# wo1's half units for both tiles two quarters at a time, and both tiles' sums ahead of the turned copies and the norm

## The chip, the cores and the metric

The kernel runs on one core of a Trainium2 chip. The metric is device time in microseconds, the median of several executions. A core has TensorE (PE, with its weight loads as PEld), VectorE (DVE), ScalarE (ACT), GpSimd (POOL) and SyncE (SP), which here issues nearly all transfers, and 16 DMA engines. Each engine runs its own program in order; they meet at semaphores.

## The reference, cut to what matters

One layer for 256 tokens of width 1024: a norm, one wide projection, three branches (chunked attention, a state-space scan, attention into a memory), their gated sum through `w_out`, and then a mixture of 32 experts, four for each token.

```python
x = x + merged @ w_out[l]
x = x + moe_ffn(rms_norm(x, norm_ffn[l]), w_router[l], b_router[l], w_gate[l], b_gate[l],
                w_up[l], b_up[l], w_down[l], b_down[l])
...
logits = (xt @ w_router + b_router).astype(jnp.float32)
top_val, top_idx = lax.top_k(logits, TOP_K)
wts = jax.nn.softmax(top_val, axis=-1)
...
g = jnp.minimum(xblk @ w_gate[e] + b_gate[e], SWIGLU_LIMIT)
u = jnp.clip(xblk @ w_up[e] + b_up[e], -SWIGLU_LIMIT, SWIGLU_LIMIT)
act = (u + 1.0) * g * jax.nn.sigmoid(SWIGLU_ALPHA * g)
y = act @ w_down[e] + b_down[e]
```

## The kernel before

**Tiles and units.** The 256 tokens are two tiles of 128 rows (`t` = 0, 1). The dense part walks through `BLOCKS`, 512-column blocks of the weights, each cut into four quarters of 256 input rows. A quarter is a unit `w`. For each unit ScalarE rounds the weights to a high part (L713), VectorE takes the rest (L1026), and TensorE multiplies in three passes, high by high, low by high, high by low (`three_passes`, L1597 to L1599), two input chunks for each tile. So a quarter is 6 matmuls of 128x512 per tile. `splits` holds four units in turn. The last two blocks, `("wo", 0)` and `("wo", 1)`, are the halves of `merged @ w_out`.

**The order.** `schedule()` writes one list of steps, `SCHED`; every engine walks through it and does the steps it knows. `at(w, ...)` puts a step behind unit `w`'s matmuls and the split of unit `w` + 3. What comes behind the list is written out by hand for each engine ("the tail").

**The seam.** Of the block wo1, TensorE does only tile 0 inside the list (`last_block`). Behind the third quarter the step `outT` turns the first half of `x_sb` (8 transposes of 128x128, L1584), behind the fourth `logits` does the first half of the router's product for both tiles (L1604), with the router matrix scaled on VectorE (L1370). Then the tail: `second_tile(q)` does tile 1's half units, each counted in `unit_used`; `turn_out(t)` turns the second half of `x_sb` for tile t; `last_logits(t)` is the second half of the router's product; `open_sum` starts a result bank with `x_sb` (L1871); `gather(t0, t1)` collects the rows of the next expert (L1864), and the counting matmuls (L1886, L1891, L1899, L1903) give each token its place.

**VectorE's tail.** `add_out(t)` adds wo1's product to `x_sb` (L1412), `take_xT(t)` copies the turned half (L1418), `norm_begin(t)` sums two partial squares and forms the variance (L1424, L942), ScalarE takes the root (`root`, L681), `choose(t)` finishes the inverse root in five small operations (L950 to L954), takes the logits (L1432) and the four largest, and `find_first(t)` marks the rows of expert 0 (L1449, L1451). Tile 0 goes through most of this before tile 1's sum is added. ScalarE forms the partial squares (L884) and the normed rows `h2` (L890, two halves for each tile), in the order tile 0, tile 1.

**The banks.** `group()` hands out three banks in turn for transposes and small products; TensorE may fill one again when VectorE has taken what was in it three groups ago.

**The experts.** 32 experts, each with six half-loads of 2 MB: gate 0 and 1, up 2 and 3, down 4 and 5. Ten slots hold them in turn; most slots lie over memory of the dense part. SyncE issues in order: expert 0's six during the dense part, then these:

```python
sp.wait_ge(unit_used, UNITS - 2)
expert_load(1, 0)
sp.wait_ge(unit_used, UNITS)
expert_load(1, 1)
expert_load(1, 2)
sp.wait_ge(sem("logits_ready"), TT)
sp.wait_ge(sem("h2_ready"), 2 * TT)
sp.wait_ge(sem("x_opened"), 2 * TT)
expert_load(1, 3)
```

Every later load (L515 on the queue) waits until TensorE has used what the slot held; the down half 4 of expert 0 frees the slot for the third load of expert 2. `expert()` on TensorE runs gate, scatter of the expert before, up (L1936 for both), gather for the next one, then down (L1974).

Of the kernel before, what the change touches and what calls it, by code (L numbers as in the profile page):

```python
# [92 lines left out]
def schedule():  # L93
# [110 lines left out]
    at(first("wo", 1) + 2, "outT")  # L204
    at(first("wo", 1) + 3, "logits")
# [45 lines left out]
def hybrid_block_kernel(nc, x, mem, g_mix, w_in, w_dt, a_gains, rel_rev, conv_w, conv_b, dt_bias, a_log, d_skip,  # L251
                        g_ssm, g_mem, w_mem_kv, x_gains, w_br_a, w_br_b, w_br_c, w_out, norm_ffn, w_router,
                        b_router, w_gate, b_gate, w_up, b_up, w_down, b_down, bias_dram, out):
    with ExitStack() as ctx:
# [420 lines left out]
        def _(act):  # L675
# [28 lines left out]
            for step in SCHED:  # L704
# [28 lines left out]
                elif kind == "take" and step[1] == "wo":  # L733
                    i = step[2]
                    cols = slice(i * NB, (i + 1) * NB)
                    for h in range(2):
# [3 lines left out]
                            .then_inc(sem("out_squares"), 1)  # L740
                elif kind == "take" and step[1:] != ("bc", 1):
# [139 lines left out]
            for t in range(TT):  # L881
# [4 lines left out]
                root(1)  # L886
                act.wait_ge(sem("second_norm"), t + 1)
# [33 lines left out]
        def _(dve):  # L921
# [39 lines left out]
            def rstd_here(dst, src, width):  # L961
# [12 lines left out]
                return last  # L974

# [17 lines left out]
            for step in SCHED:  # L993
# [366 lines left out]
                elif kind == "take" and step[1] == "wo":  # L1360
# [4 lines left out]
                    for h in range(2):  # L1365
                        n = GEMM_AT[("wo", i, h)]
                        dve.tensor_tensor(x_sb[:, h, cols], x_sb[:, h, cols], ps[:, GEMM_BANKS[n % 4], :], ALU.add)\
                            .then_inc(gemm_taken, 1)
                    dve.wait_ge(gain2_landed, 32)
                    dve.tensor_tensor(wr_sb[:], wr_sb[:], gain2_sb[:].unsqueeze(2).to_broadcast([P, KC, EXPERTS]),  # L1370
                                      ALU.mult).then_inc(sem("router_scaled"), 1)
                elif kind == "outT":
                    for c2 in range(2):
# [29 lines left out]
            across = [P, TOP_K, EXPERTS]  # L1403

            def add_out(t):

                n = GEMM_AT[("wo", 1, t)]
                if t == 0:
                    dve.wait_ge(sem("wo_first_tile"), 1)
                else:  # L1410
                    dve.wait_ge(unit_used, UNITS)
                dve.tensor_tensor(x_sb[:, t, NB:2 * NB], x_sb[:, t, NB:2 * NB], ps[:, GEMM_BANKS[n % 4], :], ALU.add)\  # L1412
                    .then_inc(gemm_taken, 1)

            def take_xT(t):

                b = group()
                dve.tensor_copy(xT[:, 4:8, t * P:(t + 1) * P], ps[:, b, :].rearrange("p (c t) -> p c t", c=4))\  # L1418
                    .then_inc(misc_taken, 1)

            def norm_begin(t):

                dve.wait_ge(sem("out_squares"), TT + t + 1)
                link(dve.tensor_tensor(ss_2[:, t:t + 1], ss_part[:, t:t + 1], ss_part[:, TT + t:TT + t + 1], ALU.add))  # L1424
                variance(rs_2[:, t:t + 1], ss_2[:, t:t + 1], D)

            def choose(t):

                inverse_root(rs_2[:, t:t + 1]).then_inc(sem("second_norm"), 1)
                dve.wait_ge(sem("second_norm"), t + 1)  # L1430
# [136 lines left out]
        def _(pe):  # L1567
# [42 lines left out]
            for step in SCHED:  # L1610
# [8 lines left out]
                elif kind == "gemm":  # L1619
# [39 lines left out]
                    if closes:  # L1659
                        n += 2  # L1660
# [405 lines left out]
```

## Time and profile before

| | us |
|---|---|
| median of 3 runs | 1451.22 |
| lowest, highest | 1450.0, 1451.28 |
| profiled execution | 1451.71 |
| its span | 1449.6 |
| TensorE busy in the span | 1425.6 |
| granted TensorE clock, mean | 0.999 |

The span is what the profile's engines cover; 2.1 us of the profiled execution lie around it. Two stages follow each other: the dense part to about 535 us, and the experts, 28.1 us each, to the end. The change lies between them, at 510 to 540 us. A row of the timeline gives the start, the duration, the engine and line, the tiles, how many records are in it, and in brackets the idle time ahead of it with what ended that. A float32 matmul has two records. Ends of matmuls are modelled and overlap, so the pitch, start to start, is what counts.

### The profile page before, as it was taken

The page shows a single profiled execution, that of the slowest core. Times are in us where ns is not written, and L with a number is a line of the kernel's source. Part 1 is how long each engine was busy: PE and PEld are TensorE (multiplying, and loading weights), DVE is VectorE, ACT ScalarE, POOL GpSimd, SP SyncE. Part 2 cuts the span into 40 slices and gives each one's busy share as a digit, 9 for nine tenths or more (in the row PEclk, how much of TensorE's full clock was granted, in tenths as well). Part 3 has the DMA queues.
Part 4 walks back from the last instruction along what each step waited for, and adds up shares of the span by engine and source line. Part 5 has one row for each costly group of instructions (what it writes and reads, how often), then busy time and mean ns, then how long its engine had stood idle before and what let it go on. Part 6 is the DMA issues. An engine that isn't in the chain of part 4 may idle for free.

```text
span 1449.6 us, 18621 instructions
## 1 busy us (share of the span) xinstructions
PE 1425.6 (98%) x7575; PEld 820.6 (57%) x7575; DVE 588.4 (41%) x1149; ACT 405.6 (28%) x601; POOL 63.3 (4%) x50
## 2 busy tenths in 40 slices
PE   6999999999999999999999999999999999999998
PEld 6998888777788864444444444444444444433433
DVE  6779788777788651211112121121212112111211
ACT  5766666556544531101010110110001011001100
POOL 5110000121100000000000000000000000000000
PEclk9999999999999999999999999999999999999999
DMA  8455544555474979999999999999999999999996
GB/s 251 156 189 174 162 136 162 194 161 169 166 272 144 365 300 417 428 428 428 427 429 429 430 427 429 428 430 428 430 427 430 428 428 429 429 429 428 429 428 287
DMA packets 74000, 491.27 MB, mean 339 GB/s; under 512 B 5264, under 2 KB 8976, under 8 KB 49376
## 3 DMA queue, kind: packets, MB, share of 16 engines
q1 hardware_dynamic: 71280, 487.57, 83.3%
q10 hardware_dynamic: 2160, 2.62, 0.6%
q8 instruction: 32, 0.52, 0.2%
q0 software_dynamic: 512, 0.43, 0.1%
q14 instruction: 16, 0.13, 0.0%
HBM read 488.93 MB, written 1.07 MB: 338 GB/s over the span
## 4 chain that ended last, share of the span: by engine, by line
PE 84%; DMA 10%; DVE 4%; ACT 1%; issue 1%; DVEq 0%; SPq 0%; ACTq 0%
PE ps L1936 26%; PE ps L1974 13%; PE ps L1597 8%; PE ps L1599 8%; PE ps L1598 8%; PE ps L1864 7%; DMA regions<-in_w_up 6%; PE ps L1584 4%; PE ps L1916 4%; DMA regions<-in_w_gate 3%; DVE regions L1172 1%; DVE splits L1026 1%; PE ps L1811 1%; PE ps L1944 1%; DMA halves<-in_w_in 1%
## 5 line engine op out<-in xcount | busy, mean ns | idle before, releaser
L1936 PE MATMUL ps<-regions,sig 128*64 128x512 f32 x2048 | 463.3, 594 | 4.8 <-DMA regions<-in_w_gate 4.6
L1936 PEld LDWEIGHTS ps<-regions,sig 128*64 128x64 f32 x2048 | 141.8, 137 | 277.6 <-issue 259.2
L1974 PE MATMUL ps<-regions,tmp 128*64 128x512 f32 x1024 | 225.1, 592 | 0.0
L1597 PE MATMUL ps<-splits,regions_r 128*128 128x512 f32 x512 | 205.8, 402 | 0.1
L1599 PE MATMUL ps<-splits,regions_r 128*128 128x512 f32 x512 | 200.1, 391 | 0.0
L1598 PE MATMUL ps<-splits,regions_r 128*128 128x512 f32 x512 | 199.8, 390 | 0.0
L713 ACT ACTIVATE splits<-halves 128x1024 fp32r<-128x1024 f32 x152 | 159.1, 1056 | 96.4 <-PE ps L1599 81.6
L1026 DVE TENSOR_TENSOR splits<-halves,splits 128x1024 fp32r<-128x1024 f32 x132 | 162.0, 1232 | 44.1 <-ACT splits L713 42.7
L899 ACT ACTIVATE work<-work 128x512 f32<-128x512 f32 x32 | 20.1, 629 | 475.8 <-DVE work L1524 475.8
L1974 PEld LDWEIGHTS ps<-regions,tmp 128*64 128x64 f32 x1024 | 71.7, 137 | 132.0 <-issue 129.6
L1864 PEld LDWEIGHTS ps<-craw,regions 128*128 128x128 f32 x1024 | 119.2, 192 | 25.6 <-issue 25.2
L1864 PE MATMUL ps<-craw,regions 128*128 128x64 f32 x1024 | 124.7, 275 | 0.4 <-DVE craw L1451 0.4
L1529 DVE TENSOR_SCALAR work<-ps 128x512 f32<-128x512 f32 x32 | 22.1, 691 | 239.8 <-PE ps L1936 239.8
L1597 PEld LDWEIGHTS ps<-splits,regions_r 128*128 128x128 f32 x512 | 96.2, 188 | 22.4 <-issue 3.9
L1599 PEld LDWEIGHTS ps<-splits,regions_r 128*128 128x128 f32 x512 | 96.1, 188 | 20.9
L1538 DVE COPY sig<-ps 128x512 f32<-128x512 f32 x32 | 22.1, 692 | 211.1 <-PE ps L1974 211.1
L1598 PEld LDWEIGHTS ps<-splits,regions_r 128*128 128x128 f32 x512 | 96.3, 188 | 18.4
L904 ACT ACTIVATE tmp<-ps 128x512 f32<-128x512 f32 x32 | 19.1, 597 | 303.1 <-PE ps L1584 303.1
L1524 DVE TENSOR_SCALAR work<-ps 128x512 f32<-128x512 f32 x32 | 22.1, 691 | 177.7 <-PE ps L1936 177.7
L1916 PE MATMUL ps<-sig,craw 64*128 64x512 f32 x264 | 65.6, 615 | 0.8 <-DVE sig L1538 0.8
L668 POOL TENSOR_TENSOR splits<-halves,splits 128x1024 fp32r<-128x1024 f32 x20 | 48.7, 2433 | 328.7 <-ACT splits L713 328.7
L1597 PE MATMUL ps<-regions_r,splits 128*128 128x256 f32 x192 | 55.3, 288 | 0.0
(299 smaller groups left out, 1188.1 us busy)
## 6 DMA issues: line engine op xcount, KB each, us to landing
regions<-in_w_gate SPq DMA_DIRECT2D x64, 2048.0 KB, 30.1
regions<-in_w_up SPq DMA_DIRECT2D x64, 2048.0 KB, 28.4
regions<-in_w_down SPq DMA_DIRECT2D x64, 2048.0 KB, 31.2
halves<-in_w_in SPq DMA_DIRECT2D x48, 1024.0 KB, 5.2
halves<-in_w_br_b SPq DMA_DIRECT2D x8, 1024.0 KB, 5.1
halves<-in_w_mem_kv SPq DMA_DIRECT2D x8, 1024.0 KB, 5.1
halves<-in_w_br_a SPq DMA_DIRECT2D x4, 1024.0 KB, 5.1
halves<-in_w_br_c SPq DMA_DIRECT2D x4, 1024.0 KB, 7.5
```

The source lines that it names most:

```text
L668: pool.tensor_tensor(lo, raw, hi.bitcast(F32), ALU.subtract).then_inc(lo_ready_pool, 1)
L713: act.activation(hi, raw, ACT.Copy).then_inc(hi_ready, 1)
L1026: dve.tensor_tensor(lo, raw, hi.bitcast(F32), ALU.subtract).then_inc(lo_ready, 1)
L1524: dve.tensor_scalar(g_sb, ps[:, G_BANK, :], LIMIT, None, ALU.min).then_inc(sem("g_ready"), 1)
L1584: return pe.transpose(dst, src, ident[:])
L1597: pe.matmul(out, lhs[0], rhs[0], start=start, stop=False, skip_group_check=True)
L1598: pe.matmul(out, lhs[1], rhs[0], start=False, stop=False, skip_group_check=True)
L1599: return pe.matmul(out, lhs[0], rhs[1], start=False, stop=stop, skip_group_check=True)
L1864: last = pe.matmul(ps[:, X_BANK, c * BLK:(c + 1) * BLK], h2[:, t, c * P:(c + 1) * P], hot[:, t], start=(t == 0 and c == 0), stop=(t == TT ...
L1916: last = pe.matmul(ps[:, ACC[2 * t + h], :], hot_wT[rows, t], yb[rows], start=False, stop=False, skip_group_check=True)
L1936: last = pe.matmul(ps[64 * h:64 * h + 64, bank, :], xgT[:, 4 * k + c], eslots[slot][:, c, h * NB:(h + 1) * NB], start=(k == 0 and c == 0), ...
L1974: last = pe.matmul(ps[64 * h:64 * h + 64, D_BANK, :], actT[:, c, 64 * k:64 * k + 64], eslots[slot][:, c, h * NB:(h + 1) * NB], start=False ...
```

## The change

In `schedule()` the half units of wo1's tile 1 enter the list, two behind the second quarter and two behind the fourth. `outT` and `logits` move behind all of wo1, and `outT` now also turns the second half for both tiles. The router scaling becomes a step of its own, earlier. `picks` on ScalarE gets a root of one column, whose result is not used. VectorE adds both tiles' sums first, then takes four copies, then finishes both norms, then chooses. ScalarE writes the normed rows behind both roots. On TensorE the second half of tile 1's logits waits until tile 0's are taken. SyncE's code is the same.

```diff
-    at(first("wo", 1) + 2, "outT")
-    at(first("wo", 1) + 3, "logits")
+    for q in range(2):
+        at(first("wo", 1) + 1, "second", q)
+        at(first("wo", 1) + 3, "second", q + 2)
+    at(UNITS, "outT")
+    at(UNITS, "logits")
+    at(first("bc", 0) + 1, "router_scale")
...
+                elif kind == "picks":
+
+                    act.activation(root_out[:, 31:32], ident[:, 0:1], ACT.Sqrt).then_inc(sem("root_warm"), 1)
...
                 root(1)
+            for t in range(TT):
                 act.wait_ge(sem("second_norm"), t + 1)
...
                 elif kind == "outT":
+                    add_out(0)
+                    norm_begin(0)
+                    add_out(1)
...
-            add_out(0)
             take_xT(0)
-            norm_begin(0)
+            take_xT(1)
+            norm_end(0)
+            norm_begin(1)
+            norm_end(1)
             choose(0)
-            add_out(1)
-            take_xT(1)
-            norm_begin(1)
             find_first(0)
             choose(1)
...
+                    turn_out(0)
+                    turn_out(1)
...
-            second_tile(0)
-            turn_out(0)
-            second_tile(1)
             last_logits(0)
-            second_tile(2)
-            second_tile(3)
-            pe.wait_ge(gemm_taken, GEMM_AT[("wo", 1, 0)] + 1)
+            pe.wait_ge(gemm_taken, GEMM_END)
             open_sum(0, 0)
-            turn_out(1)
+            pe.wait_ge(sem("logits_taken"), 1)
+            last_logits(1)
...
-            pe.wait_ge(gemm_taken, GEMM_END)
             open_sum(1, 0)
-            last_logits(1)
```

`norm_end(t)` is the inverse root that stood at the head of `choose(t)`.

On TensorE, from the last matmul of wo1 to the first gather and a little past it. `splits` are the weights, `ident` marks transposes and opened sums, `wr_sb` the router, `chosen_r` the counting, `craw` the gathers. Before:

```order
L1599 MATMUL ps<-splits,regions_r 128x512
L1871 MATMUL ps<-regions,ident 128x512
L1584 MATMUL ps<-ident,regions 128x128 x4
L1886 MATMUL ps<-chosen_r,upto_r 128x32
L1871 MATMUL ps<-regions,ident 128x512
L1604 MATMUL ps<-wr_sb,regions 128x32 x4
L1891 MATMUL ps<-chosen_r,ones_r 128x32
L1864 MATMUL ps<-craw,regions 128x64 x8
L1871 MATMUL ps<-regions,ident 128x512
L1899 MATMUL ps<-chosen_r,upto_r 128x32
```

and now:

```order
L1614 MATMUL ps<-splits,regions_r 128x512
L1599 MATMUL ps<-ident,regions 128x128 x16
L1619 MATMUL ps<-wr_sb,regions 128x32 x12
L1890 MATMUL ps<-regions,ident 128x512
L1619 MATMUL ps<-wr_sb,regions 128x32 x4
L1901 MATMUL ps<-chosen_r,upto_r 128x32
L1890 MATMUL ps<-regions,ident 128x512
L1904 MATMUL ps<-chosen_r,ones_r 128x32
L1883 MATMUL ps<-craw,regions 128x64 x8
L1890 MATMUL ps<-regions,ident 128x512
L1912 MATMUL ps<-chosen_r,upto_r 128x32
```

All transposes and router matmuls but the last group now stand behind the last wo1 matmul, where before a part of them stood between the quarters; tile 1's last router group has moved ahead of the first count.

On VectorE, from the copies of the picks on, behind the last split. `regions<-regions,ps` are the sums, `regions<-ps` the turned copies, `stat` the norm, `rt` the logits. Before:

```order
L1348 COPY cbm<-ident 32x128 x3
L1375 COPY regions<-ps 128x512 x2
L1412 TENSOR_TENSOR regions<-regions,ps 128x512
L1418 COPY regions<-ps 128x4x128
L1424 TENSOR_TENSOR stat<-stat 128x1
L942 TENSOR_SCALAR stat<-stat 128x1
L950 RECIPROCAL stat<-stat 128x1
L951 TENSOR_TENSOR stat<-stat 128x1
L952 TENSOR_TENSOR stat<-stat 128x1
L953 TENSOR_SCALAR stat<-stat 128x1
L954 TENSOR_TENSOR stat<-stat 128x1
L1432 SCALAR_TENSOR_TENSOR rt<-ps,stat,head_rows 128x32
```

and now:

```order
L1385 COPY cbm<-ident 32x128 x3
L993 TENSOR_TENSOR regions<-regions,ps 128x512
L1005 TENSOR_TENSOR stat<-stat 128x1
L950 TENSOR_SCALAR stat<-stat 128x1
L993 TENSOR_TENSOR regions<-regions,ps 128x512
L1417 COPY regions<-ps 128x512 x2
L999 COPY regions<-ps 128x4x128 x2
L958 RECIPROCAL stat<-stat 128x1
L959 TENSOR_TENSOR stat<-stat 128x1
L960 TENSOR_TENSOR stat<-stat 128x1
L961 TENSOR_SCALAR stat<-stat 128x1
L962 TENSOR_TENSOR stat<-stat 128x1
```

Both sums are ahead of all four copies, tile 0's inverse root is behind them, and tile 1's norm (another seven rows like these) comes before the first logits are taken.

On ScalarE, from the squares of wo0 on. Before:

```order
L739 ACTIVATE tmp,stat<-regions 128x512 x2
L884 ACTIVATE tmp,stat<-regions 128x512
L681 ACT_TABLE_LOAD
L681 ACTIVATE stat<-stat 128x1
L890 ACTIVATE regions<-regions,stat 128x512 x2
L884 ACTIVATE tmp,stat<-regions 128x512
L681 ACTIVATE stat<-stat 128x1
L890 ACTIVATE regions<-regions,stat 128x512 x2
```

and now:

```order
L743 ACTIVATE tmp,stat<-regions 128x512 x2
L747 ACT_TABLE_LOAD
L747 ACTIVATE stat<-ident 128x1
L891 ACTIVATE tmp,stat<-regions 128x512
L685 ACTIVATE stat<-stat 128x1
L891 ACTIVATE tmp,stat<-regions 128x512
L685 ACTIVATE stat<-stat 128x1
L898 ACTIVATE regions<-regions,stat 128x512 x4
```

The table load stands ahead of wo1's squares instead of behind them, and both roots are ahead of all four writes of normed rows.

## Rows read from the trace of the kernel before

**Rows 1.** Page, parts 1 and 2: busy us and count; GB/s moved, in 40 slices

```profile
PE 1425.6 (98%) x7575; PEld 820.6 (57%) x7575; DVE 588.4 (41%) x1149; ACT 405.6 (28%) x601; POOL 63.3 (4%) x50
...
GB/s 251 156 189 174 162 136 162 194 161 169 166 272 144 365 300 417 428 428 428 427 429 429 430 427 429 428 430 428 430 427 430 428 428 429 429 429 428 429 428 287
```

**Rows 2.** Page, part 5: busy us, mean ns, idle before and its releaser

```profile
L1936 PE MATMUL ps<-regions,sig 128*64 128x512 f32 x2048 | 463.3, 594 | 4.8 <-DMA regions<-in_w_gate 4.6
```

**Rows 3.** Chain that ended last: start us, us, what

```profile
1384.67 43.48 DMA regions<-in_w_up
```

**Rows 4.** Windows: us, PE, PEld, DVE, ACT, POOL busy, PEclk, DMA share, GB/s

```profile
520.00:522.00 2.00, 2.00 (x15) 1.73 (x13) 1.32 (x6) 0.20 (x1) 0.00 (x0) 1.00 0.00 0
562.00:563.00 1.00, 1.00 (x8) 0.39 (x6) 0.00 (x0) 0.00 (x0) 0.00 (x0) 1.00 0.80 295
```

**Rows 5.** Timeline of SyncE's DMA queue: start us, us, engine, line, transfer

```profile
521.70 3.96 SPq L515 DMA_DIRECT2D regions<-in_w_gate  x2
...
535.11 0.33 SPq L515 DMA_DIRECT2D regions<-in_w_up  x1
...
560.89 0.33 SPq L515 DMA_DIRECT2D regions<-in_w_up  x1
...
589.02 0.33 SPq L515 DMA_DIRECT2D regions<-in_w_up  x1
```

**Rows 6.** DMA view, 521 to 523, 535 to 536, 560 to 561: us to landing

```profile
regions<-in_w_gate SPq DMA_DIRECT2D x1, 2048.0 KB, 7.6
...
regions<-in_w_up SPq DMA_DIRECT2D x1, 2048.0 KB, 9.7
...
regions<-in_w_up SPq DMA_DIRECT2D x1, 2048.0 KB, 9.3
```

**Rows 7.** Timeline of PE, 510 to 535: start us, us, line, idle before

```profile
510.17 0.39 PE L1597 MATMUL ps<-splits,regions_r 128*128 128x512 f32 x1
...
514.02 0.39 PE L1599 MATMUL ps<-splits,regions_r 128*128 128x512 f32 x1
...
514.25 1.03 PE L1584 MATMUL ps<-ident,regions 128*128 128x128 f32 x8
...
524.91 0.40 PE L1599 MATMUL ps<-splits,regions_r 128*128 128x512 f32 x1
...
525.14 1.02 PE L1871 MATMUL ps<-regions,ident 128*128 128x512 f32 x2
...
527.61 1.05 PE L1604 MATMUL ps<-wr_sb,regions 128*128 128x32 f32 x8
...
528.61 1.98 PE L1864 MATMUL ps<-craw,regions 128*128 128x64 f32 x16
...
532.11 2.00 PE L1864 MATMUL ps<-craw,regions 128*128 128x64 f32 x16 [0.37 <-DVE craw L1451]
```

**Rows 8.** Timeline of DVE, 514 to 532, same columns

```profile
514.89 1.29 DVE L1375 COPY regions<-ps 128x512 f32<-128x512 f32 x2
...
525.34 0.69 DVE L1412 TENSOR_TENSOR regions<-regions,ps 128x512 f32<-128x512 f32 x1 [0.99 <-PE ps L1599]
...
527.45 0.15 DVE L1424 TENSOR_TENSOR stat<-stat 128x1 f32<-128x1 f32 x1
...
528.11 0.15 DVE L950 RECIPROCAL stat<-stat 128x1 f32<-128x1 f32 x1
...
529.07 0.25 DVE L1432 SCALAR_TENSOR_TENSOR rt<-ps,stat,head_rows 128x32 f32<-128x32 f32 x1
...
530.42 0.39 DVE L1442 TENSOR_REDUCE chosen_r<-work 128x32 fp32r<-128x128 f32 x1
...
531.58 0.19 DVE L1449 TENSOR_TENSOR rt<-ps,chosen_r 128x32 f32<-128x32 f32 x1 [0.70 <-PE ps L1899]
```

**Rows 9.** Timeline of ACT, 521 to 525, same columns

```profile
521.29 0.20 ACT L681 ACTIVATE stat<-stat 128x1 f32<-128x1 f32 x1 [1.85 <-DVE stat L942]
...
522.49 2.31 ACT L890 ACTIVATE regions<-regions,stat 128x512 f32<-128x512 f32 x2 [1.00 <-DVE stat L954]
```

More of the change, by code:

```diff
@@ L974, in rstd_here, with add_out, take_xT, norm_begin @@
                 return last
+            across = [P, TOP_K, EXPERTS]
+            def add_out(t):
+                n = GEMM_AT[("wo", 1, t)]
+                if t == 0:
+                    dve.wait_ge(sem("wo_first_tile"), 1)
+                else:
+                    dve.wait_ge(unit_used, UNITS)
+                dve.tensor_tensor(x_sb[:, t, NB:2 * NB], x_sb[:, t, NB:2 * NB], ps[:, GEMM_BANKS[n % 4], :], ALU.add)\
+                    .then_inc(gemm_taken, 1)
+            def take_xT(t):
+                b = group()
+                dve.tensor_copy(xT[:, 4:8, t * P:(t + 1) * P], ps[:, b, :].rearrange("p (c t) -> p c t", c=4))\
+                    .then_inc(misc_taken, 1)
+            def norm_begin(t):
+                dve.wait_ge(sem("out_squares"), TT + t + 1)
+                link(dve.tensor_tensor(ss_2[:, t:t + 1], ss_part[:, t:t + 1], ss_part[:, TT + t:TT + t + 1], ALU.add))
+                variance(rs_2[:, t:t + 1], ss_2[:, t:t + 1], D)
+            def norm_end(t):
+                inverse_root(rs_2[:, t:t + 1]).then_inc(sem("second_norm"), 1)
+                dve.wait_ge(sem("second_norm"), t + 1)
             dve.wait_ge(sem("masks"), 3)
@@ L1368, in _ @@
                             .then_inc(gemm_taken, 1)
+                elif kind == "router_scale":
                     dve.wait_ge(gain2_landed, 32)
@@ L1400, in _ @@
                             .then_inc(sem("br_merged"), 1)
[L1403 to L1425, printed above, removed]
             def choose(t):
-                inverse_root(rs_2[:, t:t + 1]).then_inc(sem("second_norm"), 1)
-                dve.wait_ge(sem("second_norm"), t + 1)
                 dve.wait_ge(sem("logits_ready"), t + 1)
@@ L1606, in router, with second_tile, turn_out @@
                 return last
+            def second_tile(q):
+                w = first("wo", 1) + q
+                hi, lo = quarter(w)[1:]
+                b = GEMM_BANKS[GEMM_AT[("wo", 1, 1)] % 4]
+                for c in range(2):
+                    k = 2 * q + c
+                    last = three_passes(ps[:, b, :], (mergedT[0][:, k, P:T], mergedT[1][:, k, P:T]),
+                                        (hi[:, c], lo[:, c]), k == 0, k == KC - 1)
+                last.then_inc(unit_used, 1)
+            def turn_out(t):
+                b = group()
+                pe.wait_ge(gemm_taken, GEMM_AT[("wo", 1, t)] + 1)
+                for c in range(4):
+                    last = turn(ps[:, b, c * P:(c + 1) * P], x_sb[:, t, (4 + c) * P:(5 + c) * P])
+                last.then_inc(misc_ready, 1)
             pe.wait_ge(sem("masks"), 3)
@@ L1660, in _ @@
                         n += 2
+                elif kind == "second":
+                    second_tile(step[1])
                 elif kind == "headT":
```

15 lines of the change are left out of this document (removed).

## The prediction

> **What bounds the kernel now.** I read the page first: TensorE is busy nearly all the time, and in the second half the 16 DMA engines carry 425 to 430 GB/s without a break [rows 1]. Both look full, so the share of busy time decides nothing, and the waits have to. The group of first-layer expert matmuls (L1936) sat idle for 4.6 us on transfers of w_gate [rows 2], and the chain that ended last passes through a transfer of w_up that takes 43.48 us from issue to landing [rows 3]. So the last experts wait for weights.
>
> Pace explains it. The third half-transfer of w_up's expert 2 lands at 560.89 + 9.3 = 570.2, and 175 transfers later expert 31's lands at 1384.67 + 43.48 = 1428.15 [rows 3, 5, 6]: 857.95 / 175 = 4.90 us each, 29.4 us for an expert's six. TensorE takes 589.02 - 560.89 = 28.13 us an expert [rows 5]. It starts with weights in store, gains 1.3 us per expert on the transfers, and runs out near the end. From there the end is the end of the transfer stream, and TensorE has about 4.6 us in hand. The question for any edit ahead of the experts is therefore when the stream last had nothing to do.
>
> The windows give two such places [rows 4]: nothing moves at 520 to 522, because the first load of expert 1 waits for the last quarters of wo1 and is issued at 521.70, its follower 3.6 us later [rows 5]; and a dip to 295 GB/s at 562 to 563. The dip belongs to the load issued at 560.89, when expert 0's down half frees its slot; it lands 9.3 us later, where a load that meets idle engines lands in 7.6 [rows 5, 6]. So before, the stream is all but caught up with TensorE at that point.
>
> **Part 1: the wo1 quarters.** The same 48 matmuls run. Their pitch is (514.02 - 510.17) / 17 = 0.2265 us [rows 7]. Before, 18 of them, then transposes and router matmuls stand between the rest, and the last starts at 524.91 [rows 7]. Now nothing stands between: the 24th ends at 510.17 + 23 x 0.2265 + 0.39 = 515.8, the 48th at 510.17 + 47 x 0.2265 + 0.39 = 521.2. The input is there: VectorE split the last quarter before it added wo0's sums, ahead of its copies at 514.89 [rows 8]. So the first load of expert 1 goes out at 515.8 instead of 521.70, 5.9 us earlier, and the next two at about 521.3 instead of 525.4. The fourth (k = 3) still waits for both tiles' logits, the normed rows and the opened sums, as at 535.11 before [rows 5].
>
> **Part 2: the chain from the sums to the first gather.** VectorE adds tile 1 at 521.25 (0.03 us after the last matmul, as at 525.34 before [rows 7, 8]). Then come four copies at the pitch of the pair at 514.89, 0.60 us, so the reciprocal of tile 0 starts at 521.25 + 5 x 0.60 = 524.3. It does not wait for its root. Before, ScalarE had idled for 1.85 us ahead of the root at 521.29, waiting for the variance [rows 9], so the table load ahead of that was hidden; now the load stands behind the squares of wo0, and the root is done near 520.6. Removing that load is thus worth nothing on the path. The norm of tile 0 takes 529.07 - 528.11 = 0.96 us to its end [rows 8], so tile 1's begins at 525.3; its sum-to-next step takes 529.07 - 527.45 = 1.62, so the first logits are taken at 526.9 (TensorE's first logits are ready at about 525.9: eight transposes 0.9, eight more 0.9 with a wait of 0.2 for the first copy, then router matmuls in three groups like the one of eight records, 0.9 each [rows 7]). From there the choice takes 530.42 + 0.39 - 529.07 = 1.74, to 528.6. TensorE has meanwhile waited for the taken logits (527.15) and done the second half of tile 1's (0.85, to 528.0), and now waits for the choice. Its counting matmul (0.25), then find-first, 532.11 - 531.58 = 0.53 [rows 7, 8], would give 529.45; the opened sum behind the counting matmul (0.9 [rows 7]) holds the queue to 529.7. So the first gather starts at 529.7 against 528.61 on its row, or 528.76 by the chain of waits: **1.0 us later**.
>
> Queued behind it on TensorE are an opened sum, the second count and the second gather. Tile 1's choice ends at 531.1, so it hides under the first gather and the sum behind it; the second gather comes 0.95 us later than its 532.11 [rows 7]. ScalarE's normed rows, 2.31 us for one tile [rows 9], now run as four in a row from 525.9 to 530.5, ahead of both gathers. All that follows (the gathered rows, weights, number of passes) hangs on the second gather, as before. Expert 0 and its freed slots shift by +1.0. The router scale, 0.4 us of VectorE, moves to a stretch where it waits for its next split; it had no one waiting before and has none now: 0.
>
> The bounds of this term: TensorE's own work from 521.1 to the gather adds to 7.2 us, which would end at 528.3, so the chain can cost -0.4 at the least. At the most, some eight hand-overs between engines that I priced at 0.03 to 0.1 us each cost 0.2 more each, which makes +2.6. I take +1.0, the sum.
>
> **Part 3: the transfers.** After the change, with issue times as above: expert 1's loads land at 515.8 + 7.6 = 523.4, then 521.3 + 7.6 = 528.9, then about 534. The fourth is issued at 536.1 and meets idle engines: 543.7, where it landed at 535.11 + 9.7 = 544.8 before [rows 5, 6]. So 5.9 us of an earlier start shrink to 1.1 here. The next ones follow at 4.90: 548.6, 553.5, 558.4, 563.3. The load of 560.89 is now issued at 561.9; the engines are free for it at 563.3 and it lands no sooner than 561.9 + 7.6 = 569.5 (back to back it would be 568.2). Before: 570.2. **Gain 0.7 us.** Later loads have margin: the next of this kind is issued 28.1 us later and comes to a stream that has gained backlog 1.3 us per expert. The end follows the stream: -0.7. In general it is the shift of TensorE less 1.7.
>
> The fixed part of a lone load is 7.6 - 4.90 = 2.7 us here. The Trainium skill, "DMA: Bandwidth & Descriptors", section "Anatomy of one DMA", puts it at some 2.0 us, measured on the path issued by GpSimd; by that the stream would gain 1.4 us instead of 0.7. The row decides, and these loads are issued by SyncE.
>
> **Sum.** Profiled execution 1451.71 us, span 1449.6, so 2.1 lies around it; the profiled execution stands 0.5 above the median 1451.22. Span 1449.6 - 0.7 = 1448.9; on the median, 1451.2 - 0.7 = **1450.5 us**. About 0.2% (2.9 us) is what a measurement of this kernel can tell from no change.
>
> **Rivals.**
> 1. TensorE's lateness counts in full: the earlier loads bring nothing, because the stream at the dip is paced by slots alone and the 1.7 us between 9.3 and 7.6 is how the engines drain, not a queue. The end is then +1.0: 1452.2. For it: the dip is soft, 295 GB/s and not zero. Chance 0.10, still within 0.2%.
> 2. The stream keeps the whole 5.9 us: 1445.3. That wants no new gap ahead of the fourth load and none at the slots of expert 0. Against it: both those issues hang on TensorE, which is no earlier. Partial forms of it need a seam 2 us or more shorter than my sum. Chance 0.08.
> 3. Slower: TensorE's clock falls in the seam. The change adds waits of about 0.9 and 0.6 us, in 8 us, to an engine that had none there before the 0.37 at 532.11 [rows 7]. If it fell from 2.4 to 1.2 GHz ahead of the gathers, two gathers and the sum between them, 1.85 + 0.9 + 2.0 = 4.7 us, would take twice that, TensorE would be 5.7 late, and the end 5.7 - 1.7 = +4.0: 1455.2. It decides from a lateness of 1.7 us for the sign and 4.6 for a measurable loss. Against it: the granted clock is 1.00 in the windows on both sides of the present waits [rows 4]. Chance 0.06, with the rest of what can hold the chain up by that much. The Trainium skill, "TensorE: Matmul & The Clock Gate", section "What's actually happening", says that the clock is throttled unless activity releases it; by that rule this is the case to look for.
>
> **How the numbers follow.** The forecast has 0.76, rival 1 has 0.10, rival 2 0.08, rival 3 0.06. Faster by over 0.2% is rival 2: 0.08. Slower is rival 3: 0.06. Within 0.2% is the rest: 0.86. The bounds -0.4 and +2.6 of the chain give -2.1 and +0.9 at the end, 1449.1 to 1452.1; the spread of the runs before, 1450.0 to 1451.28, and rival 1 widen this to 1448.6 to 1452.8, which leaves out rivals 2 and 3, less than 2 in 10.
>
> **What would show it.** The first load of expert 1 goes out near 515.8 and its two followers near 521.3; the DMA windows then show a new hole around 534 to 537 and a deeper one at 563; the first gather starts near 529.7 with two waits of TensorE ahead of it, for taken logits and for the choice; the pick wait of expert 0 shifts by 1.0; idle time of L1936 on w_gate shrinks from 4.6 to about 3. I am wrong if the first gather is earlier than 528 or later than 532, if the stream has no hole ahead of the fourth load, or if the clock leaves 1.00.

## The result: no gain, and two kinds of execution

| | before | after |
|---|---|---|
| median of 20 runs, us | 1450.93 | 1457.93 |
| lowest, highest | 1449.48, 1452.83 | 1450.35, 1461.44 |
| profiled execution, its span | 1451.71, 1449.6 | 1457.58, 1455.5 |
| granted TensorE clock of the profiled execution | 0.999 | 0.994 |

The ratio is 1.0036, with a 95% interval from 1.0025 to 1.0047: slower by 0.36%, clear of the noise. The ratio does not follow the medians, because the 20 runs of after are of two kinds. Seven lie between 1450.35 and 1451.44, all with a granted clock of 1.000. Thirteen lie between 1456.76 and 1461.44, all at 0.993 to 0.995. Nothing lies between. The 20 runs of before have no second kind. Three executions of the sets behind the experiments (5166.63 us in experiment 5, and 6081.64 and 8331.11 of the kernel before) took several times as long, with a granted clock of 1.0, and are left out below.

The page of after, parts 1, 2 and 5, beside [rows 1, 2]: busy time; granted clock in tenths and GB/s in 40 slices; the first expert matmuls (L1949 now) with their idle time.

```profile
PE 1432.9 (98%) x7575; PEld 826.7 (57%) x7575; DVE 588.2 (40%) x1149; ACT 405.8 (28%) x602; POOL 63.9 (4%) x50
...
PEclk9999999999999979999999999999999999999999
...
GB/s 246 158 189 173 164 136 163 189 165 174 154 271 159 356 235 422 426 430 426 431 426 430 426 430 427 430 427 429 428 428 429 428 429 427 430 427 430 427 429 297
...
L1949 PE MATMUL ps<-regions,sig 128*64 128x512 f32 x2048 | 463.5, 594 | 3.7 <-DMA regions<-in_w_gate 3.4
```

Busy time of TensorE is up by 7.3 us for the same 7575 matmuls. They did not become more, they became slower: the clock's row has a 7 in one slice, and the 15th of the GB/s row is 235 where [rows 1] have 300. The wait for w_gate, 4.6 us in [rows 2], is 3.4.

Windows of after around that slice: stretch, its length, busy time and count of PE, PEld, DVE, ACT, POOL, granted clock, DMA share, GB/s.

```profile
521.50:526.50 5.00, 4.93 (x42) 4.47 (x41) 4.26 (x13) 1.15 (x4) 0.00 (x0) 1.00 1.01 390
526.50:543.50 17.00, 16.84 (x56) 12.10 (x57) 7.12 (x34) 6.94 (x7) 0.00 (x0) 0.50 0.39 166
543.50:548.50 5.00, 5.00 (x26) 1.59 (x24) 2.84 (x16) 0.00 (x0) 0.00 (x0) 0.98 0.86 301
```

Full clock to about 526.6, half clock (1.2 instead of 2.4 GHz) for 17 us, full clock again near 543.7, once the wide expert matmuls had begun at 543.17. In the first window TensorE was busy for 4.93 of 5.00 us. What it did then is in the timeline of PE: start, duration, line, tiles, records.

```profile
521.54 2.20 PE L1599 MATMUL ps<-ident,regions 128*128 128x128 f32 x16
...
523.68 2.87 PE L1619 MATMUL ps<-wr_sb,regions 128*128 128x32 f32 x24
...
526.38 1.81 PE L1890 MATMUL ps<-regions,ident 128*128 128x512 f32 x2
...
527.98 1.76 PE L1619 MATMUL ps<-wr_sb,regions 128*128 128x32 f32 x8
...
531.68 3.65 PE L1883 MATMUL ps<-craw,regions 128*128 128x64 f32 x16
...
537.75 3.68 PE L1883 MATMUL ps<-craw,regions 128*128 128x64 f32 x16 [0.16 <-DVE craw L1467]
...
543.17 3.90 PE L1949 MATMUL ps<-regions,sig 128*64 128x512 f32 x16
```

Transposes and router matmuls of 32 columns from 521.54 to the opened sum at 526.38, then the fall, ahead of both places where the change makes TensorE wait. In this trace neither wait leaves it idle: the slowed opened sum lasts to about 527.98, past the taking of the logits (527.28 + 0.25), and the choice, done at 528.99, is there before the count at 529.54. So here the fall can't come from the two added waits. The first gather takes 3.65 where [rows 7] have 1.98, the second 3.68 instead of 2.00.

VectorE (DVE) in the same stretch: second sum, first reciprocal, first logits taken, end of the first choice.

```profile
521.74 0.69 DVE L993 TENSOR_TENSOR regions<-regions,ps 128x512 f32<-128x512 f32 x1 [0.90 <-PE ps L1614]
...
524.74 0.15 DVE L958 RECIPROCAL stat<-stat 128x1 f32<-128x1 f32 x1
...
527.28 0.25 DVE L1448 SCALAR_TENSOR_TENSOR rt<-ps,stat,head_rows 128x32 f32<-128x32 f32 x1
...
528.62 0.37 DVE L1458 TENSOR_REDUCE chosen_r<-work 128x32 fp32r<-128x128 f32 x1
```

The transfers: SyncE's queue, the landing of the load at 568.37, and the last w_up transfer of the chain.

```profile
516.28 5.77 SPq L519 DMA_DIRECT2D regions<-in_w_gate  x2
...
522.10 21.56 SPq L519 DMA_DIRECT2D regions<-in_w_up  x2
...
568.37 0.33 SPq L519 DMA_DIRECT2D regions<-in_w_up  x1
...
regions<-in_w_up SPq DMA_DIRECT2D x1, 2048.0 KB, 8.1
...
1390.53 43.48 DMA regions<-in_w_up
```

The first load goes out at 516.28, against 521.70 in [rows 5]; the fourth (the second of the pair that begins at 522.10 and lasts 21.56) near 543.3, against 535.11. Expert 0's freed slot comes at 568.37 instead of 560.89, 7.5 us late, and the last w_up lands at 1434.01 instead of 1428.15, 5.9 us late. The span grew by 5.9.

### The profile page after: what moved, and what is told of

Read it like the earlier page. It is cut to its first block, busy times and chain, and to the rows that moved or that the text cites. A ratio compares the mean times of both kernels' runs of the same rounds, so it can differ in the third digit from the quotient of the medians.

```text
span 1455.5 us, 18623 instructions
## 1 busy us (share of the span) xinstructions
PE 1432.9 (98%) x7575; PEld 826.7 (57%) x7575; DVE 588.2 (40%) x1149; ACT 405.8 (28%) x602; POOL 63.9 (4%) x50
## 4 chain that ended last, share of the span: by engine, by line
PE 85%; DMA 9%; DVE 4%; ACT 1%; issue 1%; ACTq 0%
PE ps L1949 26%; PE ps L1987 14%; DMA regions<-in_w_up 9%; PE ps L1612 8%; PE ps L1614 8%; PE ps L1613 8%; PE ps L1883 8%; PE ps L1599 4%; PE ps L1929 4%; DVE regions L1209 1%; DVE splits L1063 1%; PE ps L1847 1%; PE ps L1957 1%; PE ps L1980 1%; PE ps L1890 0%
## 5 line engine op out<-in xcount | busy, mean ns | idle before, releaser
L1949 PE MATMUL ps<-regions,sig 128*64 128x512 f32 x2048 | 463.5, 594 | 3.7 <-DMA regions<-in_w_gate 3.4
L1949 PEld LDWEIGHTS ps<-regions,sig 128*64 128x64 f32 x2048 | 142.1, 137 | 276.8 <-issue 261.3
L1883 PEld LDWEIGHTS ps<-craw,regions 128*128 128x128 f32 x1024 | 122.5, 196 | 25.9 <-issue 25.7
L1883 PE MATMUL ps<-craw,regions 128*128 128x64 f32 x1024 | 128.1, 279 | 0.2 <-DVE craw L1467 0.2
```

What stands on the lines that cost most here:

```text
L1883: last = pe.matmul(ps[:, X_BANK, c * BLK:(c + 1) * BLK], h2[:, t, c * P:(c + 1) * P], hot[:, t], start=(t == 0 and c == 0), stop=(t == TT ...
L1949: last = pe.matmul(ps[64 * h:64 * h + 64, bank, :], xgT[:, 4 * k + c], eslots[slot][:, c, h * NB:(h + 1) * NB], start=(k == 0 and c == 0), ...
```

## Experiments

The causes tested are called N, W and D in the expectations, and a fourth, L, comes in behind experiment 4. A filler is a matmul that nobody needs, put in only to give TensorE work. N: transposes and narrow matmuls for 4.9 us without wide ones take the clock down. W: the added waits of TensorE do. D: the earlier transfers do. Every median below stands beside runs of the kernel before on the same chip (1451.29 for experiments 1 to 4, 1451.38 for 5 to 8, 1451.30 for 9 to 12).

**1. Waits filled with wide matmuls**

```diff
             open_sum(0, 0)
+            filler()
             pe.wait_ge(sem("logits_taken"), 1)
             last_logits(1)
+            filler()
```

> The changed kernel with one more 512-column float32 matmul (a product nobody reads, into the bank of the last opened sum) in each of TensorE's two new waits, ahead of the one for tile 0's taken logits and ahead of the one for the choice. Theory N: TensorE's clock falls because transposes and 32-column router matmuls run for 4.9 us (521.5 to 526.4) with nothing wide between; both fillers stand behind that, so most executions still fall, median 1457 to 1461. Rival W: the waits make it fall; then the clock stays at 1.00 in all, median 1450.5 to 1452.

Measured: 1452.41 (11 runs, 1451.5 to 1454.44). Six at 1.000, 1451.5 to 1452.41, and five at 0.999, 1453.83 to 1454.44; none like the thirteen of after. The profiled one is of the six. Timeline of PE, then a window:

```profile
523.15 2.87 PE L1619 MATMUL ps<-wr_sb,regions 128*128 128x32 f32 x24
...
526.80 1.02 PE L1895 MATMUL ps<-regions,ident 128*128 128x512 f32 x2
...
528.47 1.10 PE L1895 MATMUL ps<-regions,ident 128*128 128x512 f32 x2
...
530.40 1.98 PE L1883 MATMUL ps<-craw,regions 128*128 128x64 f32 x16
...
524.00:534.00 10.00, 9.63 (x59) 7.14 (x58) 6.19 (x34) 6.12 (x7) 0.00 (x0) 1.00 0.86 369
```

The narrow stretch is that of after. As written, N has failed and W has not, but the five that take 2 us more are foreseen by neither; experiment 6 offers an explanation.

**2. The narrow stretch broken up by wide matmuls**

```diff
+                    filler()
                     turn_out(0)
                     turn_out(1)
...
-                    for t in range(TT):
-                        router(t, 0)
+                    filler()
+                    router(0, 0)
+                    filler()
+                    router(1, 0)
```

> The changed kernel with three such wide matmuls (two records of 0.45 us each) inside the narrow stretch: behind the eight transposes of outT, ahead of tile 0's and ahead of tile 1's first router group. Nothing is taken out, 2.7 us of work are added. Theory N: clock 1.00 in all executions; the seam is 1.5 to 2 us later than that of a changed kernel at full clock, so 1452 to 1454, yet some 5 us below the changed kernel's median 1457.9. Rival W: the wait for the choice is still there, so the clock falls as often and the median is 1459 or more.

Measured: 1453.2 (11 runs, 1451.93 to 1453.79), all at 1.000. One window over the seam:

```profile
521.00:531.00 10.00, 9.77 (x61) 7.27 (x59) 7.16 (x31) 6.43 (x8) 0.00 (x0) 1.00 0.99 406
```

2.7 us of needless work, and the median is 4.7 us below after's. N foresaw this, W did not, though the fillers also shorten the waits behind them, so that this run alone does not exclude W.

**3. TensorE's part of the change alone**

```diff
-    at(first("wo", 1) + 2, "outT")
-    at(first("wo", 1) + 3, "logits")
+    for q in range(2):
+        at(first("wo", 1) + 1, "second", q)
+        at(first("wo", 1) + 3, "second", q + 2)
+    at(UNITS, "outT")
+    at(UNITS, "logits")
...
                         by_columns(lambda t: x_sb[:, t], c2)
+                    turn_out(0)
...
-            second_tile(0)
-            turn_out(0)
-            second_tile(1)
             last_logits(0)
-            second_tile(2)
-            second_tile(3)
```

> The kernel before with TensorE's part of the change alone: tile 1's half units two by two behind the second and fourth quarter, then the transposes and router matmuls of the first half, tile 0's second half and its last router group, and only then an opened sum and tile 1's second half. VectorE and ScalarE keep their order. The narrow stretch is 3.9 us instead of 4.9. Theory N: the clock falls in some or most executions, those at 1456 or more, the others near 1451. Rival W: no wait for the taken logits is added, so the clock stays at 1.00. Rival D: it is the earlier start of the transfers (518 instead of 522) that takes the clock down; then it falls here too, as often as in the changed kernel.

Measured: 1459.06 (6 runs, 1455.59 to 1463.03); all six fell, three at 0.997 and three at 0.992. Timeline of PE with the idle time in brackets, then a window of the fall:

```profile
524.58 0.63 PE L1587 MATMUL ps<-ident,regions 128*128 128x128 f32 x4 [1.75 <-DVE regions L1415]
...
525.04 3.19 PE L1607 MATMUL ps<-wr_sb,regions 128*128 128x32 f32 x24
...
530.80 1.09 PE L1587 MATMUL ps<-ident,regions 128*128 128x128 f32 x4 [0.70 <-DVE regions L1415]
...
528.00:534.00 6.00, 5.29 (x14) 2.72 (x13) 4.00 (x18) 2.94 (x5) 0.00 (x0) 0.50 0.90 385
```

This order has waits of its own, 1.75 and 0.70 us for sums, which my expectation for W had overlooked. It tells that the change's order on TensorE, without VectorE's, is enough for a fall, not by which of the two ways.

**4. VectorE's and ScalarE's part, quarters interleaved as before**

```diff
-    for q in range(2):
-        at(first("wo", 1) + 1, "second", q)
-        at(first("wo", 1) + 3, "second", q + 2)
-    at(UNITS, "outT")
-    at(UNITS, "logits")
+    at(first("wo", 1) + 2, "outT")
+    at(first("wo", 1) + 3, "logits")
...
-                    add_out(0)
-                    norm_begin(0)
-                    add_out(1)
...
+            add_out(0)
+            norm_begin(0)
             take_xT(0)
+            add_out(1)
             take_xT(1)
...
-                    turn_out(0)
-                    turn_out(1)
...
+            second_tile(0)
+            turn_out(0)
+            second_tile(1)
+            second_tile(2)
             last_logits(0)
+            second_tile(3)
+            turn_out(1)
```

> The changed kernel's order on VectorE and ScalarE (both sums early, all turned copies, both roots, then both choices), with tile 1's half units put back between the transposes and router matmuls as before the change. Theory N: clock 1.00 in all, median 1450 to 1452. Rival W: TensorE still waits for tile 0's taken logits and for the choice, so the clock falls in most and the median is 1457 or more. Rival D: the transfers start as late as before the change, so no fall.

Both sums stand in the tail again, and tile 0's turned half is copied between them, so VectorE's order is the changed one only from the second sum on. Measured: 1460.54 (5 runs, 1459.27 to 1463.15), all at 0.994 or 0.995. The same views:

```profile
526.83 0.63 PE L1596 MATMUL ps<-ident,regions 128*128 128x128 f32 x4 [0.87 <-DVE regions L990]
...
530.95 1.08 PE L1616 MATMUL ps<-wr_sb,regions 128*128 128x32 f32 x8 [2.63 <-DVE rt L1442]
...
532.51 0.25 PE L1902 MATMUL ps<-chosen_r,upto_r 128*128 128x32 f32 x1 [0.48 <-DVE chosen_r L1452]
...
534.00:547.00 13.00, 12.85 (x44) 8.96 (x45) 5.48 (x27) 2.83 (x4) 0.00 (x0) 0.50 0.44 168
```

Here the wide matmuls stand between the narrow ones to 525.9, and the clock falls near 533.7, behind waits of 0.87, 2.63 and 0.48 us. So the clock also falls without the narrow stretch, in a seam with long waits, which N does not say. D is out: the first load of expert 1 goes out at 522.34, no earlier than before.

A fourth theory was made to allow for all this, and is called L: in narrow matmuls and in waits alike TensorE does little wide work, and the clock follows the two together.

**5. The waits filled with narrow matmuls**

Here `filler()` is four matmuls of 32 columns.

```diff
             open_sum(0, 0)
+            filler()
             pe.wait_ge(sem("logits_taken"), 1)
             last_logits(1)
+            filler()
```

> The changed kernel with its two new waits filled again, this time with four 32-column matmuls each (eight records, about 0.85 us, the length of the wide filler used before; their product is read by nobody). Neither wait is idle, but nothing wide is added. Theory L (the fall follows how much wide matmul work TensorE does in the seam, and waits and narrow matmuls count alike against it): the clock falls as without fillers, median 1457 to 1461. Rival W (idle time alone takes it down): the clock stays at 1.00 as with the wide fillers, median 1451 to 1453.

Measured: 1461.23 (11 runs, 1451.96 to 1464.68). Four at 1.000, 1451.96 to 1452.48, and seven at 0.991 to 0.993, 1461.22 to 1464.68. Windows, then the two fillers:

```profile
521.50:526.50 5.00, 4.93 (x42) 4.38 (x40) 4.09 (x12) 0.88 (x4) 0.00 (x0) 1.00 1.00 374
...
527.50:547.50 20.00, 19.84 (x72) 15.25 (x72) 7.24 (x32) 6.22 (x7) 0.00 (x0) 0.50 0.30 129
...
527.80 1.76 PE L1896 MATMUL ps<-wr_sb,regions 128*128 128x32 f32 x8
...
531.08 1.89 PE L1896 MATMUL ps<-wr_sb,regions 128*128 128x32 f32 x8
```

Same places as the fillers of experiment 1, no idle time left there, and seven of eleven executions are like the thirteen of after, where experiment 1 had none. In the profiled one the clock falls near 527.4, ahead of the first filler. So W is out for the order of the change: neither here nor in after does an added wait stand ahead of the fall. The Trainium skill, "TensorE: Matmul & The Clock Gate", section "What's actually happening", says that activity releases the throttle. The trace agrees only if activity is something else than the busy time of the profile, which is 4.93 of 5.00 us ahead of this fall too.

**6. One wide filler, in the first wait**

```diff
             open_sum(0, 0)
+            filler()
             pe.wait_ge(sem("logits_taken"), 1)
```

> The changed kernel with one wide 512-column float32 filler, ahead of the wait for tile 0's taken logits; the wait for the choice stays. Theory L: half the cure; executions are mixed, some fallen (1456 or more) and some not (1451 to 1452). If the first wait alone is the cause, none falls; if the second is, as many fall as in the changed kernel, 13 in 20.

Measured: 1453.3 (11 runs, 1450.95 to 1454.04): four at 1.000, 1450.95 to 1452.27, seven at 0.999, 1452.99 to 1454.04. The profiled one, of the seven, inside its fall:

```profile
527.00:530.00 3.00, 3.00 (x7) 1.33 (x5) 1.79 (x9) 3.00 (x4) 0.00 (x0) 0.50 1.02 437
```

The clock fell as in after, near 526.7 and ahead of the filler, and came back near 530 instead of at the experts. I had expected executions at 1456 or more; none came. This tells two things apart. **How often** the clock falls does not visibly change with fillers behind the narrow stretch: 13 of 20 in after, 5 of 11, 7 of 11 and 7 of 11 in experiments 1, 5 and 6, if the five of experiment 1 are read as short falls. None of those five was profiled, and their 0.999 is no sign of it: the profiled execution of before has 0.999 too, from its last stretch, 1440 to 1450 us, where the clock's mean is 0.89. What marks the five is their time. Only the fillers inside the stretch, experiment 2, brought it to 0 of 11. That fits N for the beginning of the fall in this order. **How long** it lasts goes with what comes next: with a second wide matmul beside the opened sum, 1 and 6, it costs 2 us; with a narrow one, 5, or none, after, 6 to 13.

**7. The opened sums moved into the seam**

```diff
+                    open_sum(0, 0)
                     turn_out(0)
                     turn_out(1)
...
-                    for t in range(TT):
-                        router(t, 0)
+                    router(0, 0)
+                    open_sum(1, 0)
+                    router(1, 0)
...
             last_logits(0)
-            pe.wait_ge(gemm_taken, GEMM_END)
-            open_sum(0, 0)
+            open_sum(0, 1)
...
-            open_sum(1, 0)
...
             gather(0, 1)
-            open_sum(0, 1)
+            open_sum(1, 1)
...
             gather(1, 2)
-            open_sum(1, 1)
```

> The changed kernel with its own four opened sums (wide matmuls that it has to do in any case) moved into the seam: one behind the eight transposes of outT, one between the two first router groups, one ahead of the wait for the taken logits, one behind the first gather. No work is added or taken away. Theory L: clock 1.00 in all, median 1450.3 to 1451.8, and 6 us below the changed kernel. Rival W: the wait for the choice stays, so some executions fall.

Measured: 1455.06 (9 runs, 1452.7 to 1456.7), two at 0.999 and seven at 0.995 to 0.997. Missed: I had looked at the first light stretch only. Timeline of PE and a window:

```profile
526.47 1.10 PE L1644 MATMUL ps<-regions,ident 128*128 128x512 f32 x2
...
529.45 2.00 PE L1890 MATMUL ps<-craw,regions 128*128 128x64 f32 x16 [0.46 <-DVE craw L1467]
...
531.29 1.88 PE L1644 MATMUL ps<-regions,ident 128*128 128x512 f32 x2
...
532.00:541.00 9.00, 7.98 (x29) 5.23 (x29) 4.38 (x22) 1.28 (x1) 0.00 (x0) 0.50 0.63 237
```

The sums taken forward are missing behind the first choice. Between the sum at 526.47 and the next one at 531.29 there are only narrow matmuls and waits of 0.24 and 0.46, and the clock falls at 531.4 instead of 526.6. The light stretch had been moved, not removed. The nine at 0.995 to 0.999 end 1.3 to 5.3 us above the kernel before; only this one of them was profiled.

**8. The kernel before, with the transfers held back**

```diff
             sp.wait_ge(unit_used, UNITS - 2)
+            sp.wait_ge(sem("logits_ready"), TT)
             expert_load(1, 0)
```

> The kernel before, with SyncE's first load of expert 1 held back until both tiles' logits are there (issued at about 528.7 instead of 521.70). TensorE's order and clock are those of before. Theory S (the stream of transfers, from the last place where it ran dry, sets the end): that load lands at 536.3, the fourth at 551.0 instead of 544.8, and the stream is 6.2 us late from there on: 1457. Rival P (the stream is paced by freed slots alone, and when it starts is of no account): 1451, no change.

Measured: 1457.31 (5 runs, 1456.71 to 1457.89), clock 1.000: +5.9 us, 1457 expected. Issue and landing of the fourth load, and the first expert matmuls:

```profile
535.30 0.33 SPq L515 DMA_DIRECT2D regions<-in_w_up  x1
...
regions<-in_w_up SPq DMA_DIRECT2D x1, 2048.0 KB, 16.8
...
L1937 PE MATMUL ps<-regions,sig 128*64 128x512 f32 x2048 | 463.8, 595 | 8.2 <-DMA regions<-in_w_gate 7.7
```

It lands at 552.1 instead of 544.8, and the experts wait 7.7 us for w_gate instead of 4.6. The stream does set the end, and of the 7.3 us by which that load lands later, 5.9 are paid.

**9. The table load alone, on the kernel before**

```diff
+                elif kind == "picks":
+                    act.activation(root_out[:, 31:32], ident[:, 0:1], ACT.Sqrt).then_inc(sem("root_warm"), 1)
```

> The kernel before with one part of the change alone: ScalarE takes a root of one column behind the squares of wo0, which moves the table load ahead of wo1's squares. The prediction priced this at 0, since the load was hidden behind the wait for the variance: no change, clock 1.00, 1451.3 within 1 us. A rival would say that a hidden load still cost 1.3 us: 1450.

Measured: 1451.59 (11 runs, 1450.64 to 1452.45), ratio 1.0004, interval 0.9995 to 1.0012. Timeline of ACT:

```profile
514.75 1.28 ACT L743 ACT_TABLE_LOAD   x1
...
521.37 0.20 ACT L681 ACTIVATE stat<-stat 128x1 f32<-128x1 f32 x1 [3.14 <-DVE stat L945]
```

The load moved to 514.75; the root still waits for the variance and runs at 521.37, against 521.29 in [rows 9].

**10. One sum early, one wide filler in its place**

```diff
+                    open_sum(0, 0)
                     turn_out(0)
                     turn_out(1)
...
             last_logits(0)
-            open_sum(0, 0)
+            filler()
             pe.wait_ge(sem("logits_taken"), 1)
```

> The changed kernel with tile 0's first opened sum moved up behind the eight transposes of outT (it needs only wo0's sums) and one wide filler where it stood, ahead of the wait for the taken logits; the other three opened sums stay between and behind the gathers. Theory L: light work in no stretch lasts as long as in the changed kernel, so the clock stays at 1.00 or falls only briefly; 1451 to 1453. Against it: as many falls as with the one filler alone (8 in 11, brief).

Measured: 1456.89 (6 runs, 1452.41 to 1460.94): two at 0.999, 1452.41 and 1452.67, and four at 0.994 or 0.995. Missed. (Of experiment 6, seven in 11 were the slower ones, not eight.) It does as much wide work as experiment 6, but one piece of it stands 4 us earlier, so that one wide matmul follows the narrow stretch instead of two together, as in after and experiment 5, and like those it has long falls. The profile is of one of the two mild executions, so where the others fell is not seen. This one did not fall at all in the seam; its 0.999 comes from the end, as in before:

```profile
521.50:550.00 28.50, 26.74 (x153) 15.30 (x153) 15.70 (x64) 9.11 (x12) 0.00 (x0) 1.00 0.83 335
1440.00:1450.00 10.00, 5.15 (x24) 1.52 (x20) 2.07 (x3) 1.19 (x2) 0.00 (x0) 0.93 0.28 106
```

**11. The kernel before, its first opened sums late**

```diff
-            open_sum(0, 0)
             turn_out(1)
...
-            open_sum(1, 0)
             last_logits(1)
...
             open_sum(1, 1)
+            open_sum(0, 0)
+            open_sum(1, 0)
```

> The kernel before, with nothing of the change: only the opened sums of the first halves, two wide matmuls of 0.9 us between the narrow ones at 525 to 528, stand behind the second gather now. The same work, in another order, and about 1.8 us less ahead of the gathers. Theory L: the clock falls in most executions, at about 528 to 532, and these end at 1455 or more. If the fall belongs to something else in the change (the order of the wo1 quarters, the early transfers, the new wait), the clock stays at 1.00 and the time at 1450 to 1452.

Measured: 1456.51 (5 runs, 1455.85 to 1457.74), all at 0.995 or 0.996. Timeline of PE and a window:

```profile
526.66 0.63 PE L1584 MATMUL ps<-ident,regions 128*128 128x128 f32 x4 [0.87 <-DVE regions L1412]
...
528.16 1.05 PE L1604 MATMUL ps<-wr_sb,regions 128*128 128x32 f32 x8 [0.86 <-DVE regions L1418]
...
529.16 2.84 PE L1864 MATMUL ps<-craw,regions 128*128 128x64 f32 x16
...
531.00:540.00 9.00, 8.85 (x29) 6.67 (x29) 3.16 (x14) 3.64 (x4) 0.00 (x0) 0.50 0.83 353
```

Nothing of the change is in it: the order of the quarters, the first three loads of expert 1 (522.19 and 526.19 at the head of their rows) and the waits for logits are those of before. Only the fourth load, which waits for all opened sums, goes out later, at 541.98, and that is 12 us behind the fall. Two wide matmuls that stood between narrow ones are gone from there, waits of 0.87 and 0.86 us open in their place, and the clock falls at about 530.1 in the profiled execution. The other four are at 0.995 or 0.996 too. So the kernel before kept its clock by the place of these two sums. Whether as wide work or by covering the waits, this run does not tell.

**12. The changed kernel once more**

> The changed kernel once more, for a profile: with the clock fallen (13 of 20 executions) the first gather starts near 531.7 and the second at 537.8; with the clock at 1.00 (7 of 20), by the prediction's sum, the first gather starts at 529.7 plus the shift of the dense part, the second 3.4 us later, and the time is about 1451.

Measured: 1458.76 and 1459.92, clock 0.993 and 0.994. The profiled one, row of PE and windows on both sides of the fall:

```profile
522.91 3.21 PE L1619 MATMUL ps<-wr_sb,regions 128*128 128x32 f32 x24
...
520.80:525.20 4.40, 4.33 (x38) 3.91 (x36) 4.02 (x12) 0.72 (x2) 0.00 (x0) 1.00 1.01 395
...
525.30:545.70 20.40, 20.25 (x66) 13.69 (x67) 8.94 (x45) 7.36 (x8) 0.00 (x0) 0.50 0.43 169
```

The clock falls near 525.3, amid the router matmuls, with the first opened sum (525.93) and both waits still to come. Both executions fell, so there is no trace of the changed kernel at full clock.

## Why the prediction was wrong

**The step that failed** is the weight of rival 3. Every duration of the sum was taken at full clock, on the ground that the clock was 1.00 on both sides of the present waits. That ground was beside the point: the change takes away the wide matmuls between the narrow ones, and none of the rows showed such a seam. The prediction looked for the danger in idle time (waits of 0.9 and 0.6 us) and gave it 0.06. In both traces of the changed kernel the fall begins in or just behind the narrow stretch, ahead of those waits (526.6 and 525.3), and it struck 13 of 20 executions and both of the later ones. So what the clock's fall does to the end was foreseen, what brings it about was not.

**Its price was too small**: +4.0 against +5.9 in the profiled pair. I had doubled two gathers and the sum between them, 4.7 us. The fall began ahead of the router group and the counts and lasted over the last opened sum and part of the first expert matmuls; TensorE was 7.5 us late at expert 0's freed slot where the working had 5.7. The rule that turned this into the end, lateness less 1.7 us, gave 7.5 - 1.7 = 5.8 against 5.9. So near a hit is partly luck: the load at that slot landed in 8.1 us and not in 7.6, and over all the traces the rule is looser, as shown below.

**What held, read from after's own rows.** The 48 matmuls without a gap: the transposes begin at 521.54, 0.5 later than by the sum, since the dense part ended that much later in this execution. With the sum's figure in brackets: first load at 516.28 (515.8), reciprocal at 524.74 (524.3), logits taken at 527.28 (526.9), choice ending at 528.99 (528.6): each about 0.1 us or less from the sum once the 0.5 is counted. Table load worth nothing: experiment 9. Lone load in 7.6 us: the one at 536.9 in experiment 1 lands in 7.5.

**The transfers: slack, but no gain shown.** The prediction took the 1.7 us between 9.3 and 7.6 for a queue that earlier loads would shorten. By how much expert 0's freed slot comes later than in before (560.89), and by how much the span grows (1449.6 before):

| profiled execution | first load goes out | slot later | span longer | difference |
|---|---|---|---|---|
| experiment 2 | 514.65 | 1.4 | 1.5 | -0.1 |
| experiment 1 | 515.76 | 1.8 | 0.7 | 1.1 |
| experiment 6 | 516.31 | 3.2 | 1.9 | 1.3 |
| experiment 11 | 522.19 | 5.9 | 4.1 | 1.8 |
| after | 516.28 | 7.5 | 5.9 | 1.6 |
| experiment 4 | 522.34 | 10.2 | 8.8 | 1.4 |

The other five traces (experiments 3, 5, 7, 10 and 12) give 0.7 to 1.4. So lateness mostly does not count in full, against rival 1. But experiment 2, with the earliest loads, saves nothing, and experiments 4 and 11, whose loads start as late as in before, save as much as the rest. The saving is slack that before has at that slot already, and no row shows that starting the loads 5.9 us earlier bought anything. At full clock the changed kernel is level with before: median 1451.09 for its seven executions against 1450.93, mean 1450.93 against 1451.05, where the forecast had -0.7. With so few executions and no trace of one, this second step of the sum stays unproven rather than refuted. Rival 2 did not occur.

**What stays open.** The order decides how often the clock falls, but the same kernel does both: 7 and 13, 4 and 7, 2 and 4. What differs from one execution to the next no run shows. That the five slower executions of experiment 1 are short falls is argued from their 2 us, not seen. Theory L is the account that fits these experiments best, not a proven rule: what it forecast missed in 6 (milder than expected), 7 and 10 (worse), and how much wide work is enough, and where, no run shows.

No version came out ahead of the kernel before. The best of those with the change's order, experiment 6 in its four executions at full clock and the changed kernel in its seven, are level with it.

## What to carry to other kernels

Before small matmuls, transposes and waits are gathered into one stretch, ask what kept TensorE's clock up there; a busy row does not tell, the granted clock does, and a trace of the old order says nothing of the new one. In this kernel the wide work that was due anyway belonged between the narrow (experiment 11), and taking it from one place opened the next (experiment 7): look at every light stretch up to the next dense one. And run such a change many times: where executions are of two kinds, a few runs tell little of how often each comes.

## What the runs showed of the hardware

The granted clock fell from 2.4 to 1.2 GHz with TensorE busy 4.93 of 5.00 us, on transposes of 128 columns and router matmuls of 32, and stayed there for 17 us of gathers of 64 columns, router matmuls, opened sums and counts. The Trainium skill, "TensorE: Matmul & The Clock Gate", section "HAM oscillation — how this bites in real kernels", gives the rule as one against idle gaps of TensorE; here the clock fell with hardly any (0.07 us in that window), and experiment 5, with the gaps filled by narrow matmuls, fell in 7 of 11. For this seam the measurement decides: gaps filled with narrow matmuls did not help, and wide ones in the same gaps kept all 11 executions at 1454.44 or less. Experiment 4, whose fall follows waits of 0.87, 2.63 and 0.48 us, shows that gaps are not harmless either.
